# A hybrid decoder layer on one core: the two layer norms and the first four slabs behind them, done token tile by token tile

## What is computed

```python
h = layer_norm(ALPHA * h + 0.5 * swiglu(h, ffn1...), ln1_g, ln1_b)
mix = hybrid_mixer(h, positions, w_in, ...)          # begins with proj = h @ w_in
h = layer_norm(ALPHA * h + mix, ln2_g, ln2_b)        # mix ends with merged @ w_out
h = layer_norm(ALPHA * h + 0.5 * swiglu(h, ffn2...), ln3_g, ln3_b)

def layer_norm(x, g, b):
    mu = mean(x); xc = x - mu; var = mean(xc * xc)
    return xc * rsqrt(var + 1e-5) * g + b
```

## Time and profile before

| | |
|---|---|
| median of 3 runs | 2665.34 us (2665.28 to 2666.05) |
| the profiled execution: its time / its span | 2665.07 us / 2663.5 us |
| TensorE matmul busy | 2637.9 us, 99% of the span |
| VectorE / ScalarE / GpSimd busy | 1997.0 / 1367.6 / 125.8 us |
| mean granted TensorE clock | 0.998 |
| HBM read | 506.23 MB, 192 GB/s over the span |

### The profile page before, as it was taken

How to read it: one execution, slowest core, us unless ns; L and a number is a source line. 1 busy time by engine, 2 the same in 40 slices (tenths; PEclk the granted TensorE clock), 3 DMA queues, 4 the chain that set the end, 5 groups by cost and what they waited for, 6 DMA issues and landing times.

```text
span 2663.5 us, 36821 instructions
## 1 busy us (share of the span) xinstructions
PE 2637.9 (99%) x12614; PEld 2193.2 (82%) x12614; DVE 1997.0 (75%) x2394; ACT 1367.6 (51%) x1686; POOL 125.8 (5%) x170
## 2 busy tenths in 40 slices
PE   9999999999999999999999999999999999999997
PEld 7888888888787788888888888888888888888886
DVE  6999997688666665677777765444779999977986
ACT  5555555455444554566555554444355555554553
POOL 1000000000000000211111100000000000000000
PEclk9999999999999999999999999999999999999999
DMA  7666566666655556665555565667666666666664
GB/s 224 198 197 205 189 203 207 213 198 201 197 173 146 155 150 198 206 181 180 177 177 175 179 183 165 192 191 245 204 194 202 190 211 187 204 202 231 213 205 172
DMA packets 286468, 513.98 MB, mean 193 GB/s; under 512 B 19664, under 2 KB 53120, under 8 KB 284320
## 3 DMA queue, kind: packets, MB, share of 16 engines
q1 hardware_dynamic: 279824, 485.03, 58.2%
q0 software_dynamic: 4880, 25.36, 2.6%
q10 hardware_dynamic: 1664, 2.26, 0.2%
HBM read 506.23 MB, written 6.36 MB: 192 GB/s over the span
## 4 chain that ended last, share of the span: by engine, by line
PE 96%; DVE 3%; ACT 1%; issue 0%; DMA 0%; POOL 0%; POOLq 0%; ACTq 0%; SPq 0%; DVEq 0%
PE acc L798 13%; PE acc L800 13%; PE acc L799 13%; PE acc L865 5%; PE acc L867 5%; PE acc L866 5%; PE acc L885 5%; PE acc L883 5%; PE acc L884 5%; PE spare L883 4%; PE spare L885 4%; PE spare L884 4%; PE spare L867 3%; PE spare L866 3%; PE spare L865 3%; PE spare L767 2%
## 5 line engine op out<-in xcount | busy, mean ns | idle before, releaser
L1751 DVE TENSOR_TENSOR w_lo<-land,w_hi 128x1024 fp32r<-128x1024 f32 (+1 forms) x956 | 1151.2, 1221 | 503.7 <-ACT w_hi L1324 495.4
L1324 ACT ACTIVATE w_hi<-land 128x1024 fp32r<-128x1024 f32 (+1 forms) x956 | 976.7, 1028 | 912.8 <-PE acc L800 320.0
L798 PE MATMUL acc<-w_hi,a_hi 128*128 128x512 f32 (+1 forms) x1184 | 450.4, 380 | 2.1 <-DVE w_lo L1751 1.2
L800 PE MATMUL acc<-w_hi,a_lo 128*128 128x512 f32 (+1 forms) x1184 | 435.1, 368 | 0.0
L799 PE MATMUL acc<-w_lo,a_hi 128*128 128x512 f32 (+1 forms) x1184 | 433.7, 366 | 0.0
L798 PEld LDWEIGHTS acc<-w_hi,a_hi 128*128 128x128 f32 x1184 | 223.4, 189 | 46.2 <-issue 9.8
L800 PEld LDWEIGHTS acc<-w_hi,a_lo 128*128 128x128 f32 x1184 | 223.2, 189 | 38.1
L799 PEld LDWEIGHTS acc<-w_lo,a_hi 128*128 128x128 f32 x1184 | 223.7, 189 | 37.2 <-issue 3.6
L865 PE MATMUL acc<-w_hi,a_hi 128*128 128x512 f32 x576 | 226.7, 393 | 1.9 <-DVE w_lo L1751 1.0
L867 PE MATMUL acc<-w_hi,a_lo 128*128 128x512 f32 x576 | 224.5, 390 | 0.0
L866 PE MATMUL acc<-w_lo,a_hi 128*128 128x512 f32 x576 | 224.2, 389 | 0.0
(11 more groups left out here) (392 smaller groups left out, 4242.7 us busy)
## 6 DMA issues: line engine op xcount, KB each, us to landing
land<-w_in SPq DMA_DIRECT2D x232, 512.0 KB, 3.9
land<-ffn_w_gate SPq DMA_DIRECT2D x176, 512.0 KB, 3.8
land<-ffn_w_up SPq DMA_DIRECT2D x176, 512.0 KB, 4.2
land<-ffn_w_down SPq DMA_DIRECT2D x176, 512.0 KB, 4.6
land<-w_ssd_o SPq DMA_DIRECT2D x64, 512.0 KB, 4.2
land<-w_in SPq DMA_DIRECT2D x132, 128.0 KB, 2.3
land<-w_attn_o SPq DMA_DIRECT2D x32, 512.0 KB, 4.1
land<-w_out SPq DMA_DIRECT2D x32, 512.0 KB, 4.5
```

The lines of the kernel that those rows point to most:

```text
L798: pe.matmul(to, rows_hi, hi, start=first, stop=False)
L800: mm = pe.matmul(to, rows_lo, hi, start=False, stop=last)
L1324: act.activation(w_hi[:, l % SPLIT, 0:deep, 0:width], land[:, l % LAND, 0:deep, 0:width], ACT.Copy).then_inc(high, 1)
L1751: dve.tensor_tensor(w_lo[:, l % SPLIT, 0:deep, 0:width], land[:, l % LAND, 0:deep, 0:width], w_hi[:, l % SPLIT, 0:deep, 0:width].bitcast(F ...
```

## The change

Four slabs (`HEAD = 4`) behind either norm are now run for tile 0 first and then for tile 1, and everything ahead of them goes by tile.

- GpSimd, behind each root, normalises the two pieces of 512 columns of that tile itself (`tensor_scalar`, 128x512, in place); VectorE no longer does. Columns 1024 to 2047 stay on VectorE.
- TensorE turns tile 0's units 0 and 1 between the last two slabs ahead of the norm, units 2 and 3 behind them. No identity is turned any more in the seams.
- ScalarE makes each unit's high part for one tile at a time: 2 activations of 128 elements and a copy of 256, eight times in a seam instead of four times 256, 256 and 512. All four first slabs are copied to `w_hi` in this part.
- VectorE makes `a_lo` for one tile at a time (256 elements, eight times), and the low parts of slabs 0 and 1 ahead of tile 1's statistics, of slabs 2 and 3 between tile 0's units.
- TensorE runs six matmuls each for tile 0 of slabs 0 to 3, turns tile 1's units meanwhile, then six each for tile 1, with the turns of units 4 to 7 behind them.
- The three DMAs for `head_r` stand behind all eight units of the first seam in ScalarE's list.

```diff
             def deviations(no):
...
                 for t in range(TOK):
                     pool.wait_ge(ln_v, (no - 1) * TOK + t + 1)
-                    reciprocal_root(rstd[:, t:t + 1], mv[:, t, 1:2], 1).then_inc(ln_p, 1)
+                    root = reciprocal_root(rstd[:, t:t + 1], mv[:, t, 1:2], 1)
+                    if no == 3:
+                        root.then_inc(ln_p, 1)
+                        continue
+                    ch.link(root)
+                    for c in range(2):
+                        part = resid[:, t, c * W:(c + 1) * W]
+                        pool.tensor_scalar(part, part, mv[:, t, 0:1], rstd[:, t:t + 1], ALU.subtract, ALU.mult
+                                           ).then_inc(ln_x, 1)
...
@@ last_slabs (down does the same behind its slabs 42 and 43)
                         if t == 1:
                             mm.then_inc(used, 1)
+                            if s >= n_slabs - 2:
+                                u = 2 * (s - n_slabs + 2)
+                                ln_turn_tile(ln, x_no, 0, (u, u + 1))
...
-            def ln_turn_first(phase, x_no):
+            def head_slabs(phase, ln, x_no, no):
                 for t in range(TOK):
-                    for u in range(4):
-                        ln_turn_half(phase, u, x_no, t)
-                    keep_clock(WARM_GAP[t])
+                    for l in range(HEAD):
+                        if t == 0:
+                            pe.wait_ge(rest, slab_no(phase, 0, l) + 1)
+                            pe.wait_ge(first_low, (no - 1) * HEAD + l + 1)
+                        else:
+                            wait_bank(ln, 0, f"t{l}")
+                        for k in range(2):
+                            rows = tuple(m[:, 2 * l + k, t * P:(t + 1) * P] for m in (a_hi, a_lo))
+                            block = tuple(m[:, l % SPLIT, k, :] for m in (w_hi, w_lo))
+                            mm = three(acc[:, t, :], rows, block, l == 0 and k == 0, False)
+                        if t == 1:
+                            mm.then_inc(used, 1)
+                            ln_turn(ln, l + HEAD, x_no)
+                        elif l >= HEAD - 2:
+                            ln_turn_tile(ln, x_no, 1, (2 * (l - HEAD + 2), 2 * (l - HEAD + 2) + 1))
...
@@ ScalarE
+            def head(after, ln, cols, no):
+
+                split(after, 0, 0)
+                split(after, 0, 1)
+                head_tile(ln, 0, cols, 0, no)
+                split(after, 0, 2)
+                head_tile(ln, 1, cols, 0, no)
+                split(after, 0, 3)
+                head_tile(ln, 2, cols, 0, no)
+                head_tile(ln, 3, cols, 0, no)
+                for u in range(HEAD):
+                    head_tile(ln, u, cols, 1, no)
...
@@ VectorE
-            def ln_first(phase, i, cc, scale, no, after):
-
-                for t in range(TOK):
-                    evacuate_half(phase, i, cc, scale, t, no)
-                    dve.wait_ge(ln_p, (no - 1) * TOK + t + 1)
-                    ln_part(t, 0)
-                    ln_part(t, 1)
-                    if t == 0:
-                        for l in range(EARLY_V):
-                            split(after, 0, l)
+            def ln_first(phase, i, cc, scale, no, after, ln):
+
+                evacuate_half(phase, i, cc, scale, 0, no)
+                split(after, 0, 0)
+                split(after, 0, 1)
+                head_low(ln, 0, 0, no)
+                evacuate_half(phase, i, cc, scale, 1, no)
+                head_low(ln, 1, 0, no)
+                split(after, 0, 2)
+                head_low(ln, 2, 0, no)
+                split(after, 0, 3)
+                head_low(ln, 3, 0, no)
+                dve.wait_ge(ln_x, (no - 1) * TOK * NC_D + 4)
+                ln_chunk(2)
+                head_low(ln, 0, 1, no)
+                head_low(ln, 1, 1, no)
+                ln_chunk(3)
+                head_low(ln, 2, 1, no)
+                head_low(ln, 3, 1, no)
```

More of the change, by code:

```diff
@@ L995, in up_first @@
                 phase = f"up{f}"
-                for l in range(16):
+                if f == 2:
+                    pe.wait_ge(acc_out[0], uses_before(phase, 0))
+                    head_slabs(phase, ln, x_no, 2)
+                for l in range(0 if f == 1 else HEAD, 16):
                     if l < 8:
@@ L1073, in slab_of_heads @@
                 mm.then_inc(used, 1)
-            ln_turn_first("ln1", 0)
-            for l in range(12):
+            pair, use = acc_use("kvdt", 0, 0)
+            if use:
+                pe.wait_ge(acc_out[pair], use)
+            head_slabs("kvdt", "ln1", 0, 1)
+            for l in range(HEAD, 12):
                 if l < 8:
@@ L1357, in ln_tile, with head_tile @@
                     return
-                scaled = a_hi[:, 2 * u:2 * u + 2, :]
-                if u < SCALED_BY_ACT:
+                for k in range(2):
+                    last = act.activation(a_hi[:, 2 * u + k, :], two_tiles(bank)[:, k, :], ACT.Identity,
+                                          scale=ln_col[:, cols, 2 * u + k:2 * u + k + 1],
+                                          bias=ln_col[:, cols + 1, 2 * u + k:2 * u + k + 1])
+                last.then_inc(tile_hi, 1)
+            def head_tile(phase, u, cols, t, no):
+                if t == 0:
+                    act.wait_ge(first_turned, (no - 1) * HEAD + u + 1)
+                    bank = SPARE[phase][1][u][1]
+                    if u >= 2:
+                        act.wait_ge(first_low, (no - 1) * HEAD + u - 1)
+                else:
+                    bank = bank_ready(phase, 0, f"t{u}")
@@ L1421, in up_first @@
                         silu_plain(f, 0)
-                    if not (f == 2 and l < EARLY):
-                        split(phase, 0, l)
+                    split(phase, 0, l)
             def up_plain(f, i):
@@ L1507, in _ @@
             ffn(1, "xT", None)
-            for l in range(EARLY):
-                split("kvdt", 0, l)
+            head("kvdt", "ln1", 0, 1)
             act.wait_ge(used, slab_no("down1", 1, 43) + 1)
@@ L1727, in _ @@
                 split("out", 0, l)
-            for l in range(EARLY):
-                split("up2", 0, l)
+            head("up2", "ln2", 2, 2)
             ffn(2, "ln2", 2)
@@ L1986, in up_first @@
                 phase = f"up{f}"
-                for l in range(16):
+                for l in range(0 if f == 1 else HEAD, 16):
                     if l < 8:
                         ln_tile(ln, l, cols)
-                        if cols is not None and l in (0, 1):
-                            ln_chunk(l + 2)
                     if f == 1 and l == 7:
@@ L2000, in up_first @@
                         mixed_rows(f, ln, s)
-                    if not (f == 2 and l < EARLY_V):
-                        split(phase, 0, l)
+                    split(phase, 0, l)
                 mixed_low(f, len(SEVEN) - 1)
@@ L2194, in rotate @@
                 return last
-            for l in range(12):
+            for l in range(HEAD, 12):
                 if l < 8:
                     ln_tile("ln1", l, 0)
-                    if l in (0, 1):
-                        ln_chunk(l + 2)
-                if l >= EARLY_V:
-                    split("kvdt", 0, l, *((W, 2) if l < 8 else (4 * HEADS, 1)))
+                split("kvdt", 0, l, *((W, 2) if l < 8 else (4 * HEADS, 1)))
                 if l == 11:
```

89 lines of the change are left out of this document (48 added, 41 removed).

## The result

Over 20 runs each the changed kernel takes 2668.88 us (2668.05 to 2669.62) and the kernel before 2665.44 us (2665.06 to 2666.24): a ratio of 1.0012 with a 95% interval of 1.0007 to 1.0018, 3.4 us slower. I forecast 2660.3 with a range of 2658.0 to 2664.5. The profiled execution has a span of 2666.5 us against 2663.5. The kernel moved by less than the 0.2% that I took as the line for "same", to which I had given 0.48. But the ratio's interval lies wholly above 1, the kernel went the other way than forecast, and the time lies 4.4 us above the range.

A forecast was written before the change was run, and what follows sets the result against it. TensorE, busy for 99% of the span, was taken as the bound. Gains of 3.1 us in the second seam and 1.9 in the first summed to 5.0, giving a median of 2660.3 us, range 2658.0 to 2664.5.

The forecast's parts named there:

- GpSimd's piece: GpSimd normalising 512 columns in the seams: 1.04 us by itself, 1.35 us beside VectorE; range ends 0.75 and 2.3 us.
- a seam without the loads: The second seam, where ScalarE issues no `head_r` loads: 3.1 us gained.
- VectorE and GpSimd beside each other: Tile 0's pieces overlap the low parts of slabs 0 and 1: 1.35 us a piece, low parts losing half the overlap.
- the wait ahead of slab 43: TensorE, before the old stage's last slab: turns wait for GpSimd's first piece from 716.47 until 716.75.
- GpSimd and VectorE hold each other up: Rival, chance 0.15: stretched pieces delay TensorE ahead of slab 43; 2.0 and 1.0 us gain remain, 2662.3 us.
- Loads of `head_r`: First seam, ScalarE: three loads taking 1.36 us now stand behind the eighth unit; 1.9 us gained there.
- ScalarE's units: ScalarE in the seams: 0.8 us for the activation pair and 0.42 for the copy, 1.25 us a unit, eight times.
- TensorE's clock: Rival, chance 0.08: without identity turns, bursts and gaps lower TensorE's clock in the heads, giving 2671 to 2682 us.
- Stores and landings: GpSimd's four stores, some 3 us later, meet the loads of slabs 4 to 7, at no cost.

The follow-up runs named there:

- e4: The changed kernel, but VectorE waits for both of GpSimd's pieces of tile 0 before making the low parts of slabs 0 and 1: 2670.84 us, one run.
- e1: The changed kernel with the pieces normalised on VectorE again, GpSimd making only the root, the order by tile kept: 2661.47 us.
- e3: The changed kernel with the pieces back on VectorE and the `head_r` loads issued by SyncE: 2660.11 us.
- e2: The changed kernel with the three `head_r` loads issued by SyncE instead of ScalarE, the pieces still on GpSimd: 2666.75 us.
- e7: The kernel before, without the 22 transposes of the identity in each seam: 2668.58 us.
- e10: The changed kernel with pieces on VectorE (tile 1's behind slab 2's low part), `head_r` loads on SyncE, GpSimd normalising columns 1024 to 2047: 2661.51 us.
- e9: The changed kernel with GpSimd's pieces computed with two constants instead of each row's mean and root: 2665.47 us, one run.
- e6: The changed kernel with GpSimd's pieces cut to one operation, subtracting the mean without the product with the root: 2666.11 us, one run.
- e8: The kernel before, in its old order, with GpSimd making the root and the two pieces of each tile: 2671.42 us.

## Why the prediction was wrong

- **GpSimd's piece, the step that failed.** "The new one reads one tensor but does two operations with pointer scalars, so I take 1.04", stretched to 1.35: it takes 2.07 with nothing beside it (e4), 2.47 in tile 0 and 2.72 in tile 1. The neighbours I bounded it by, a copy and a two-input operation, were other instructions, and the upper end that I kept for the range, 2.3, lies below the 2.47 and 2.72 measured. With the price undone (e1, e3) the seams come out at -2.63 and -2.48 against the -3.1 that I gave for a seam without the loads.
- **VectorE and GpSimd beside each other.** The direction was right, the shape was not. I stretched both pieces of tile 0 by 1.3; measured, one piece of a tile bears it all, from 2.07 to 2.87 us in tile 0 (1.39) and to 3.37 in tile 1 (1.63), and the other none. The mean for tile 0, 1.19, is below my 1.3 all the same. Of the two low parts one went from 1.2 to 1.58 us. What I didn't price at all was tile 1: its first piece, and its root, 1.43 us instead of 0.57 where VectorE makes slab 2's low part beside it.
- **The list of waits.** I put the wait ahead of slab 43 at 0.3 us; it was 1.80. It moves the last slab of the old stage, tile 1's statistics, its root and its pieces, so it counts in full. A second wait of 1.21 us, for tile 1's first piece, I had at nothing. With both waits gone (e1) the seams are 3.99 and 3.45 us shorter than in the change. The rival "GpSimd and VectorE hold each other up" named the mechanism, with the wait ahead of slab 43, but said that at 3 us a piece nothing is lost; measured, 2.5 to 2.7 us a piece lose 0.82 a seam, as the second root is late too.
- **Loads of `head_r`.** The mechanism was right (the first seam is the worse one, by these loads): I gave them 1.2 us of the path; e2 shows 1.39 and e3 0.73. That they take 2.33 us to issue in the change was a surprise.
- **ScalarE's units.** 1.25 us each by tile: right (0.81 + 0.42), and the pairs of activations too.
- **TensorE's clock.** It didn't fall in the change, as forecast with 0.92. But my reason, that idle time of 1.9 us cost no clock before, left out that the turns of the identity were what kept it up; e7 shows that they were. Nor was my sentence right that by the Trainium skill the time would be the rival's: the section I named has waits that are longer than the runs between them, and I forecast bursts of 1.4 us with gaps of 0.8.
- **Stores and landings.** No wait on them shows in TensorE's or ScalarE's list in the seams, as forecast.

## What to carry to other kernels

Work that is moved to another engine costs that engine's price, and a row of another instruction of the same size isn't a bound for it: measure the very instruction once, or keep a factor of two in the range. Ask first whether the engine that is relieved was late at all; here VectorE stood idle for 3.13 us while it waited for the engine that had been given its work. And where a part of a list is cut into tiles, look at what else stands in it: three DMA issues on ScalarE that waited in idle time before became 1.4 us of the path.

## What the runs showed of the hardware that I had not expected

- GpSimd's `tensor_scalar` on 128x512 float32 takes 1.56 us with one operation, 1.92 with two constants, 2.07 with two pointer scalars; a two-input operation of that size takes 1.04, and VectorE needs 0.5 for the same piece.
- GpSimd's `pow` on one element a partition takes 0.57 us, and 1.43 beside a low part on VectorE, an operation that has two inputs. It starts 0.2 us after the low part started and ends 0.42 us after the low part ended, in e4 and e10 too, as if it had waited for it.
- Not every overlap costs. In e9 the pieces of tile 1 took 1.93 us in both seams, hardly more than the smallest (1.92), beside a slab's low part that took 1.21 us and so was not stretched either. What decides it is left open.
- Three DMA issues on ScalarE took 1.36 us in the kernel before and 2.33 behind three stores that GpSimd had issued in a row. In the same place they took 2.17 us in e4, 2.95 in e6 and 2.20 in e9, and 1.37 in e1, where the stores come singly. Why is left open; no run varied the stores alone.
- Waits of up to 1.8 us between groups of six matmuls left TensorE's granted clock at 1.00 in the change; a wait of 2.42 us, 8 turns and the start of another wait took it to 0.50 in both seams of e7. The waits alone don't settle it: in e4 and in e8 the two seams have all but the same waits ahead of the place, and the clock fell in the first and stayed up in the second.
